# Rearranging VectorE's work inside the RWKV scan: cleared buffers moved from GpSimd, products and masked copies in another order

## The reference, cut to what matters

```python
def step(S, inp):
    r_t, w_t, k_t, v_t, kk_t, a_t = inp
    sa = jnp.einsum('bhvk,bhk->bhv', S, -kk_t)
    S = (S * w_t[:, :, None, :] + sa[..., None] * (kk_t * a_t)[:, :, None, :]
         + v_t[..., None] * k_t[:, :, None, :])
    return S, jnp.einsum('bhvk,bhk->bhv', S, r_t)
```

## Time and profile before

| | us |
|---|---|
| median of 3 runs (4257.63 to 4261.09) | 4258.85 |
| the profiled execution | 4261.09 |
| its span | 4259.3 |
| PE busy | 3707.2 (87%) |
| DVE busy | 2197.1 (52%) |
| ACT busy | 1036.5 (24%) |
| POOL busy | 832.1 (20%) |

### The profile page before, as it was taken

One profiled execution on the slowest core, in us unless ns is written; L12 is line 12 of the kernel. 1 busy time (PEld: TensorE's weight loads), 2 busy tenths in 40 slices (PEclk: granted clock), 3 DMA queues, 4 the chain that ended last, 5 costly groups with the idle time before them and its releaser, 6 DMA issues.

```text
span 4259.3 us, 52319 instructions
## 1 busy us (share of the span) xinstructions
PE 3707.2 (87%) x21059; PEld 2037.7 (48%) x21059; DVE 2197.1 (52%) x4392; ACT 1036.5 (24%) x2734; POOL 832.1 (20%) x892
## 2 busy tenths in 40 slices
PE   7988898999989677777777777699999999899999
PEld 4555565898844233323333222455554444444444
DVE  4856534787545776776776544533331027533311
ACT  1422221444311222322322322311110012411100
POOL 1033301445200433333333333000000000000000
PEclk8989998899899899999999999899999999999999
DMA  4146520000021999999999999311111111012212
GB/s 163 59 181 236 206 72 8 3 3 3 34 82 49 414 420 420 420 420 418 420 412 411 420 420 420 122 37 43 60 40 54 54 44 60 1 60 77 68 68 74
DMA packets 167089, 743.01 MB, mean 174 GB/s; under 512 B 12022, under 2 KB 58369, under 8 KB 91840
## 3 DMA queue, kind: packets, MB, share of 16 engines
q0 software_dynamic: 77264, 549.79, 31.3%
q1 hardware_dynamic: 89008, 187.77, 12.4%
q10 hardware_dynamic: 576, 2.10, 0.1%
HBM read 737.52 MB, written 2.10 MB: 174 GB/s over the span
## 4 chain that ended last, share of the span: by engine, by line
PE 56%; DMA 19%; DVE 10%; ACT 3%; issue 1%; POOL 0%; DVEq 0%; POOLq 0%; ACTq 0%
PE bank L104 31%; DMA row<-in_experts,idxs 10%; PE bank L2646 9%; DMA wring<-in_experts,idxs 9%; PE bank L2627 6%; DVE junk L2532 2%; PE bank L974 1%; PE bank L955 1%; PE bank L1699 1%; PE bank L1673 1%; PE bank L1689 1%; PE bank L2904 0%; DVE TT L1022 0%; DVE TTm L1016 0%; ACT dg L2603 0%
## 5 line engine op out<-in xcount | busy, mean ns | idle before, releaser
L104 PE MATMUL bank<-h2T,wring 128*128 128x512 f32 (+1 forms) x2112 | 759.3, 522 | 0.0
L2627 PE MATMUL bank<-row,dg 128*128 128x512 f32 x1224 | 590.5, 630 | 187.6 <-ACT dg L2603 187.4
L104 PEld LDWEIGHTS bank<-h2T,wring 128*128 128x128 f32 x2112 | 402.3, 191 | 355.6 <-issue 337.4
L2532 DVE CUSTOM_DVE_ANT_0 junk<-row,bank 128x1024 f32<-128x1024 f32 x306 | 373.7, 1221 | 251.7 <-DMA row<-in_experts,idxs 238.1
L2627 PE MATMUL bank<-wring,dg 128*128 128x512 f32 x824 | 393.2, 624 | 118.7 <-ACT dg L2603 118.6
L2627 PEld LDWEIGHTS bank<-row,dg 128*128 128x128 f32 x1224 | 233.9, 199 | 543.1 <-issue 542.9
L2646 PE MATMUL bank<-wring,gT 128*128 128x512 f32 x880 | 382.0, 597 | 8.6 <-DVE gT L3044 8.6
L2518 POOL DMA_INDIRECT row<-in_experts,idxs x306 | 295.1, 964 | 474.8 <-PE bank L2627 468.3
L2532 DVE CUSTOM_DVE_ANT_0 junk<-wring,bank 128x1024 f32<-128x1024 f32 x206 | 251.6, 1221 | 174.5 <-DMA wring<-in_experts,idxs 166.8
L2627 PEld LDWEIGHTS bank<-wring,dg 128*128 128x128 f32 x824 | 156.4, 198 | 353.4 <-issue 353.3
L3033 DVE TENSOR_SCALAR cv<-pad,fp 128x769 f32<-128x769 f32 (+1 forms) x88 | 54.2, 615 | 509.3 <-ACT pad L2999 509.3
(11 more groups left out here) (546 smaller groups left out, 5020.2 us busy)
## 6 DMA issues: line engine op xcount, KB each, us to landing
wring<-in_ada_w SPq DMA_DIRECT2D x36, 2048.0 KB, 8.4
wring<-in_ffn_w_up SPq DMA_DIRECT2D x44, 1024.0 KB, 7.6
wring<-in_ffn_w_down SPq DMA_DIRECT2D x8, 2048.0 KB, 7.9
wring<-in_w_in SPq DMA_DIRECT2D x7, 2048.0 KB, 8.0
wring<-in_peer_w_query SPq DMA_DIRECT2D x4, 2048.0 KB, 7.8
wring<-in_ffn_w_down SPq DMA_DIRECT2D x4, 1536.0 KB, 6.7
wring<-in_attn_w_qkv SPq DMA_DIRECT2D x3, 2048.0 KB, 7.9
row<-in_experts,idxs POOLq DMA_INDIRECT x306, 17.6
```

Of the source, the lines that this page charges most:

```text
L104: ins = e.matmul(out, l, r, start=(start and n == 0), stop=(stop and n == len(pairs) - 1))
L2532: e.tensor_tensor_reduce(self.junk, self.ring[j % self.ROWS][:, 0:1024], P.pairs[b % 2], 1.0, 0.0, MUL, ADD, self.dots[:, b % 2, x:x + 1]) ...
L2627: ins = e.matmul(ks[half], self.dg[u % 4], self.ring[u % self.ROWS][:, 1024 + half * 512:1536 + half * 512], start=(x == 0), stop=(x == 127))
```

## The change

Three things, all in the scan:

1. The memsets leave POOL. `zero_po` is gone, and DVE clears the same buffers itself at the head of units 0, 1, 6 and 7, before the first step of the inversion.
2. The fourth part of prepare (`be` times `ka2`, and `ka2` from `kd`) moves from ahead of level 3 to behind `state_dv`, ahead of level 4; and the product for `rho` becomes a part of its own, behind level 4.
3. The masked copies of Qb, which stood ahead of level 4, move behind it and behind `rho`; those of Qk follow as before.

```diff
             if u % 6 < 2:
-                dv.wait_ge(*P.at("r_zero", u))
+                for q in range(2):
+                    for n in ("TT", "BT", "Qb", "Qk"):
+                        e.memset(self.res[u % 2][q][n], 0.0).then_inc(*V.up())
+                dv.wait_ge(*V.now())
...
             if u:
                 self.y_dv(dv, u - 1)
-            next(make, 0)
             self.levels_dv(dv, u, 3)
             if u:
                 self.state_dv(dv, u - 1)
+            next(make, 0)
+            self.levels_dv(dv, u, 4)
+            next(make, 0)
             if x:
                 self.keep_dv(dv, u, "Qb")
-            self.levels_dv(dv, u, 4)
-            if x:
                 self.keep_dv(dv, u, "Qk")
             self.levels_dv(dv, u, 5)
...
-        self.zero_po(po, 0)
-        self.zero_po(po, 1)
...
-            if u in (5, 6):
-                self.zero_po(po, u + 1)
...
         e.tensor_tensor(w["ka2"], tmp["kd"], w["ka2"], MUL).then_inc(*V.up("r_ops_bk", u))
+        yield
         if b >= 2:
             e.tensor_tensor(w["rho"], p.rT[:, :, blk], w["rho"], MUL).then_inc(*V.up())
```

## The result

| | median us | executions | ratio to before, 95% |
|---|---|---|---|
| before | 4259.97 | 4 | |
| after | 4312.16 | 4 (4298.58 to 4320.46) | 1.0114 [1.008, 1.0149] |

The forecast was 4277 with a range of 4266 to 4294. Three of the four executions of before lie within 3.5 us, the fourth is at 4271.5. 119 more, taken beside the experiments, have medians of 4267 to 4271 in five groups and go from 4244 to 4294. So before takes some 10 us more than the few runs of the forecast showed, and the change costs 37 us in the means (4308.1 over five executions against 4271.0 over 119): against the larger base it is twice the forecast, not three times. Two executions in a slow state are left out everywhere, one of before (12801.8 us, granted clock 0.485) and one of memsets (4965.5 us, 0.732).

A forecast was written before the change was run, and what follows sets the result against it. TensorE was taken to bound the output units (busy 33.48 of 34.00 us). Terms -6.0 + 9.9 - 2.9 + 1.2 + 14.7 + 1.3 = +18.2 us on 4261.09 gave 4279.3, or 4277 as median; range 4266 to 4294.

The forecast's parts named there:

- The start, -6.0: Start of the scan: without POOL's memsets the `lw` scaling and the work to P finish sooner, -6.0 us.
- Memsets, +9.9: Memsets on DVE: hidden in unit 0, 3.3 us each in units 1, 6 and 7, together +9.9 us.
- Level 3 earlier, -2.9: Level 3 no longer waits for the two moved products: 1.8 us in unit 0, 1.1 in unit 6.
- level 4 later, +1.2: Units 1 and 7: the two products now stand between state and level 4, +0.7 and +0.5 us.
- The stall, +14.7: Seven output units: PE waits for the moved Qb copy ahead of turned `be`, 2.5 us each, less reliefs: +14.7 us.
- reliefs: Taken off the stall's 17.5 us: 0.8 since unit 5 has no `rho`, 2.0 for the Qk product's vanished state waits.
- The sum at equal clock, +18.2: All terms of the scan added, with no term for the clock: +18.2 us.
- the forecast's own range: The main case, without a rival coming true: 4271 to 4284 us, chance 0.67.
- The clock: Rival: half clock follows the new gaps, a 3.4 us dip at each of seven stalls; +8 to +16 us, chance 0.16.
- the bank was not free: Rival that Qb's bank is free anyway, so turned `be` causes no stall: +3.5 us, 4262; chance 0.04.
- VectorE was not the bound: Rival that VectorE bounds all twelve units and the reordering pays: -18 us, 4241; chance 0.04.
- The half clock of unit 2: Rival that unit 2's half-clock stretch goes as starts move: -7.8 us, 4269; chance 0.09.

The follow-up runs named there:

- memsets: Before, with only the memsets moved to DVE at the head of units 0, 1, 6 and 7 and `zero_po` gone; median 4279 us, ratio 1.001.
- nocopies: The whole change, but with the copies of Qb left ahead of level 4; median 4305 us, ratio 1.0081.
- products: Before, with only the two products moved behind the state and `rho` behind level 4; median 4275 us, ratio 1.0016.
- The four corners: Half clock: before 410 us; Qb copies moved (seven stalls) 478; two idle products at L983 of each unit 371; both 381.
- the idle products: Two full-size TensorE products, results unused, ahead of each unit's second L983 group; added to before: 4260 us, 0.9976; added to start: 4255 us, 0.997.
- start: Before, with unit 0's memsets on DVE, unit 1's later on POOL, and products moved in units 0 and 6 only; median 4259 us, ratio 0.9971.
- pad4: Before, with the four turned products of `be` issued twice in seven output units; median 4276 us, ratio 1.0016.
- start_tight: The start kernel with level 5 on DVE ordered as both Tm steps, then TT; median 4253 us, ratio 0.9976.
- copies_fill: Before, with only the copies of Qb moved behind level 4, plus three idle products in each of the seven stalls; median 4306 us, ratio 1.0085.
- fill: The whole change plus five idle products on TensorE ahead of turned `be` in the output units; median 4309 us, ratio 1.0085.

## Why the prediction was wrong

Term by term:

- *The start, -6.0.* Right. P was done 4.71 us after the scaling of `lw` began (721.74 + 1.41 - 718.44), where it was 10.93 (735.06 + 1.63 - 725.76), 6.2 less, and the wait for `ka` fell from 16.2 to 9.9 us, 6.3.
- *Memsets, +9.9.* Hidden in unit 0, as forecast. In units 1, 6 and 7 L965 waits 6.7 us in all (memsets kernel), against some 9 forecast. In the profile the part as a whole came out as forecast (+3.9), in the mean some 6 us cheaper, for a reason that stays open.
- *Level 3 earlier, -2.9, and level 4 later, +1.2.* In unit 0 level 3 follows `be` at once (748.13 against 746.99 + 1.22). `ka` is waited for 1.2 us in each of units 1 and 7: that is where I see the second term, and it is twice as large as I had it (2.3 instead of 1.2).
- *The stall, +14.7.* The waits are 14.7 us in 7 places, 2.2 at most where I had 2.3 to 2.8: before reliefs I had 16.7. The main relief came on top, since no wait for S is left (1.8 in the earlier trace rows). So this term was 12.9 net, 1.8 under the forecast.
- *The sum at equal clock, +18.2.* Measured +14.6 ± 1.9 over the executions and +15.7 in the scan of the profile (40.8 - 65.7 x 0.382). Both lie inside the forecast's own range, 12 to 25 over its base of 4259. That the sum came so close is in part luck: memsets alone cost 6 us less than forecast, and nocopies 6 us more than memsets and products together.
- *The clock: the step that failed.* I left it out of the sum and made it a rival with a chance of 0.16, at +8 to +16 us. It came: 59 us more at half clock on average (469 against 410), x 0.382 = +22 us; in the profiled scan 65.7, +25. So the step that failed is the one that put the clock at nothing in the sum. The rival's price per us was right, its size was not: I counted one short dip of 3.4 us behind each stall. There are four of those in the output units; the rest are long stretches, up to 27 us, that begin elsewhere. My argument against it (ten waits without half clock behind each) looked at waits one by one. The four corners show that for the stalls it is a wait and what stands behind it that count together.
- *The base.* The three executions behind 4259 lie 12 us under the mean of 119, 1.6 standard errors of three (12.6 us for one), so chance can account for it. Some 10 us of the 52 in the first table come from there, and nothing in the mechanism.

Of the other rivals, the bank was not free and VectorE was not the bound. The half clock of unit 2 did shrink (34.3 us at 0.95 instead of 39.50 at 0.74), as that rival said, while five other units gained more than it lost.

**What stays open.** Why one and the same gap is followed by half clock in one unit and not in the next; why memsets and products together raise it more than each; why the idle products bring so little on top of start; and whether a single full-size product would do what two did. What about L983 matters, the gap or the small products, was not tried apart: the gap was never removed, since its wait is for a bank that VectorE still reads. Nor were the idle products tried with the memsets alone or with the whole change, so what they would give back there is not shown.

## What to carry to other kernels

Where the clock of TensorE changes inside a kernel, write it into the sum as a term: new waits in a stretch where it is busy can cost more than their length, here 26 us of clock on 14 us of waits. Time the kernel before often enough to know its spread (here 50 us), and judge changes by the mean clock of many executions, with the price per us at half clock fitted from them, since a single trace of pad4 or start_tight would have told the opposite. And before a masked copy is moved back in a queue, look up who needs its bank next: that part of the sum could be read to a few us from rows alone.

## What the runs showed of the hardware

- The granted clock stayed at 1.2 GHz (0.50) for up to 17 us while PE was busy without a pause (unit 10 of after, from 1090.0 to 1106.5: 16.50 of 16.50 us busy), and for 27 us with short ones (from 1171.5 on, 25.3 of 27.5 us busy). In these stretches busy time alone did not bring 2.4 GHz back.
- 24 full-size idle products (128x128; 48 rows beside the scan's 8400), two in each of 12 places, took 39 us of half clock away, and 97 with the stalls. In the stalls themselves 21 (copies_fill) took 14 ± 11 us and 35 (fill) none. The Trainium skill (TensorE: Matmul & The Clock Gate, "HAM oscillation — how this bites in real kernels") puts the fall of the clock down to idle gaps. The trace agrees in part: the stalls, which are idle time, cost 68 us at half clock. But shortening them from 1.6 to 1.0 us brought nothing that shows, and the gain came from work put at L983, where the gap stayed at 0.53 us.
- The memset on VectorE (0.48 us) was as long beside POOL's masks (unit 1 of after) as with POOL idle (unit 0), while the scaling of `lw` took 5.71 us beside POOL's memsets and 0.43 without them. The Trainium skill (SBUF — State Buffer, "Who interferes with whom") says of such a scaling that it and GpSimd can block each other, and the trace agrees with 5.71 against 0.43.
